# Stick-breaking attention: score matmuls two heads ahead, in pairs over four PSUM banks

## What is computed

```python
z = jnp.einsum('bhqd,bhkd->bhqk', qb, kb).astype(jnp.float32) * scale
mask = k_pos < q_pos
log_keep = jnp.where(mask, jax.nn.log_sigmoid(-z), 0.0)
after = lax.cumsum(log_keep, axis=3, reverse=True) - log_keep
w = jnp.where(mask, jnp.exp(jax.nn.log_sigmoid(z) + after), 0.0)
outs.append(jnp.einsum('bhqk,bhkd->bhqd', w.astype(vb.dtype), vb))
```

## Time and profile before

| | us |
|---|---|
| median of 3 runs | 1062.97 |
| lowest, highest | 1062.87, 1064.98 |
| span of the profiled execution | 1061.0 |
| TensorE busy | 1022.0 (96%) |
| VectorE busy | 690.2 (65%) |
| ScalarE busy | 621.5 (59%) |
| scores of the heads, first and last start | 501.1, 582.5 |

### The profile page before, as it was taken

How to read it: one execution, slowest core, us unless ns; L and a number is a source line. 1 busy time by engine, 2 the same in 40 slices (tenths; PEclk the granted TensorE clock), 3 DMA queues, 4 the chain that set the end, 5 groups by cost and what they waited for, 6 DMA issues and landing times. The chain is left out here.

```text
span 1061.0 us, 16887 instructions
## 1 busy us (share of the span) xinstructions
PE 1022.0 (96%) x6975; PEld 919.7 (87%) x6975; DVE 690.2 (65%) x981; ACT 621.5 (59%) x952; POOL 126.1 (12%) x119
## 2 busy tenths in 40 slices
PE   6999998999999999999999999999999989999997
PEld 5999897988998888789888799999889969899995
DVE  5788676867865687786566564545557886545554
ACT  6779676655664666375666654344456965443443
POOL 1010059440200122530000000000000100000000
PEclk9999999999999999899999999999999999999999
DMA  9885255433677432246332375565554355555540
GB/s 338 303 264 174 68 167 189 159 121 95 197 246 268 160 119 81 80 138 214 125 120 80 120 236 178 181 199 176 181 159 159 119 159 199 199 183 179 193 159 40
DMA packets 116476, 178.41 MB, mean 168 GB/s; under 512 B 5204, under 2 KB 74098, under 8 KB 116400
## 3 DMA queue, kind: packets, MB, share of 16 engines
q1 hardware_dynamic: 115136, 174.23, 50.1%
q0 software_dynamic: 1120, 2.97, 0.9%
q10 hardware_dynamic: 144, 0.13, 0.0%
HBM read 176.27 MB, written 1.05 MB: 167 GB/s over the span
## 5 line engine op out<-in xcount | busy, mean ns | idle before, releaser
L1484 DVE TENSOR_TENSOR sb_w_lo<-sb_raw,sb_w_hi 128x2048 fp32r<-128x2048 f32 (+1 forms) x139 | 309.4, 2227 | 194.3 <-ACT sb_w_hi L776 194.1
L776 ACT ACTIVATE sb_w_hi<-sb_raw 128x2048 fp32r<-128x2048 f32 (+1 forms) x134 | 254.2, 1900 | 135.4 <-PE G L2332 106.3
L2330 PE MATMUL X<-sb_hT_hi,sb_w_hi 128*128 128x256 f32 x784 | 222.9, 284 | 1.4 <-DVE sb_w_lo L1484 0.8
L2331 PE MATMUL X<-sb_hT_lo,sb_w_hi 128*128 128x256 f32 x784 | 221.3, 282 | 0.0
L2332 PE MATMUL X<-sb_hT_hi,sb_w_lo 128*128 128x256 f32 x784 | 221.2, 282 | 0.0
L2330 PEld LDWEIGHTS X<-sb_hT_hi,sb_w_hi 128*128 128x128 f32 x784 | 149.4, 190 | 3.3 <-issue 0.9
L2331 PEld LDWEIGHTS X<-sb_hT_lo,sb_w_hi 128*128 128x128 f32 x784 | 149.4, 191 | 0.7
L2332 PEld LDWEIGHTS X<-sb_hT_hi,sb_w_lo 128*128 128x128 f32 x784 | 149.4, 191 | 0.0
L2330 PE MATMUL G<-sb_w_hi,sb_uT_hi 128*128 128x512 f32 x304 | 121.0, 398 | 3.2 <-DVE sb_uT_lo L2265 1.6
L2332 PE MATMUL G<-sb_w_hi,sb_uT_lo 128*128 128x512 f32 x304 | 120.1, 395 | 0.0
L2331 PE MATMUL G<-sb_w_lo,sb_uT_hi 128*128 128x512 f32 x304 | 120.0, 395 | 0.0
(11 more groups left out here) (508 smaller groups left out, 1971.6 us busy)
## 6 DMA issues: line engine op xcount, KB each, us to landing
sb_raw<-in_mlp_w SPq DMA_DIRECT2D x64, 1024.0 KB, 5.2
sb_raw<-in_ada_w SPq DMA_DIRECT2D x22, 1024.0 KB, 5.4
sb_raw<-in_b_in_w SPq DMA_DIRECT2D x16, 1024.0 KB, 5.7
sb_raw<-in_a_in_w SPq DMA_DIRECT2D x14, 1024.0 KB, 6.6
sb_raw<-in_sb_w_qkv SPq DMA_DIRECT2D x12, 1024.0 KB, 5.1
sb_raw<-in_rg_w_in SPq DMA_DIRECT2D x8, 1024.0 KB, 5.3
sb_raw<-in_a_out_w SPq DMA_DIRECT2D x4, 1024.0 KB, 5.1
sb_raw<-in_b_out_w SPq DMA_DIRECT2D x4, 1024.0 KB, 5.3
```

The costliest lines, as they stand in the source:

```text
L776: nc.scalar.activation(split_tile(w_hi, m)[:, 0:nk * w], raw_of(b)[:, 0:nk * w], ACT.Copy).then_inc(S["w_hi"], 1)
L1484: ins = nc.vector.tensor_tensor(split_tile(w_lo, m)[:, at], raw_of(b)[:, at], split_tile(w_hi, m)[:, at].bitcast(F32), ALU.subtract)
L2330: dt32(out, lh, rh, start=first, stop=False, skip_group_check=shared)
L2331: dt32(out, lh, rl, start=False, stop=False, skip_group_check=shared)
```

## The change

Scores are issued two heads ahead and in pairs. `z_scores(h)` now serves heads h and h + 1: first both 256-column matmuls, then both 128-column ones, then both masks. The table `SB_AHEAD` says at the top of which iteration which pair is issued: pairs 2, 4, 6, 8, 10 at heads 0, 2, 4, 6, 8, pair 12 at head 11, pair 14 at head 12; pair 0 goes ahead of the whole V block. The banks are G0, G1, T0, T1 in turn for heads 0 to 11 and G0 to G3 for heads 12 to 15 (`z_bank`). As T0, T1, G2 and G3 are also the outputs of `sb_o`, its pieces wait for the weights of heads 10, 11, 14 and 15. The table of pieces gives the heads from 10 on fewer: one each for heads 10 to 14, pieces 28 and 29 behind the sums of head 15, and 30 and 31 behind the last product. On ScalarE the weights of head h - 1 come in iteration h, behind the high part of h and the softplus of h + 1; the two V copies of the start come behind the softplus of head 1. Splits, reads and the `o2` steps move by an iteration; the last `sb_read` stands at head 11, ahead of `z_first(12)`.

```diff
@@ -44,9 +44,11 @@
 SB_FIRST, SB_LATER = (0, 4, 1, 5), (2, 6, 3, 7)
-SB_PIECES = (3, 3, 3, 2, 2, 2, 2, 2, 2, 2, 2, 2, 2, 1, 1, 1)
-SB_SPLITS = (1, 2, 4, 6, 8, 10, 12)
-SB_READ = (2, 3, 9, 10)
+SB_PIECES = (3, 3, 3, 2, 2, 2, 2, 2, 2, 2, 1, 1, 1, 1, 1, 0)
+SB_SPLITS = (2, 3, 5, 7, 9, 11, 15)
+SB_READ = (2, 3, 9)
+SB_LAST_READ = 11
+SB_AHEAD = {0: 2, 2: 4, 4: 6, 6: 8, 8: 10, 11: 12, 12: 14}
...
@@ -492,6 +494,9 @@
...
             return (qS if n < 4 else kS)[:, 2 * (n % 4):2 * (n % 4) + 2, :], HD ** -0.5 if n < 4 else 1.0
+
+        def z_bank(h):
+            return (G[0:2] + TB)[h % 4] if h < 12 else G[h - 12]
...
@@ -1289,7 +1294,7 @@
...
                     act.wait_ge(S["sb_pv"], h - 1)
-                nc.scalar.activation(ws[h % 2][:, :, :], G[h % 2][:, 0:384].rearrange("p (c n) -> p c n", c=3),
+                nc.scalar.activation(ws[h % 2][:, :, :], z_bank(h)[:, 0:384].rearrange("p (c n) -> p c n", c=3),
...
@@ -1305,21 +1310,24 @@
...
             ch.link(nc.scalar.activation(neg_r[:, :], const("neg_ones"), ACT.Copy))
-            sb_values(0, 0)
             z_softplus(0)
-            sb_values(0, 1)
-            split_for(first_mm["sb_v"] + 1)
...
                     z_softplus(h + 1)
-                sb_weights(h)
-                if h in (5, 7):
-                    sb_values(1, (h - 5) // 2)
+                if h == 0:
+                    sb_values(0, 0)
+                    sb_values(0, 1)
+                    split_for(first_mm["sb_v"] + 1)
+                else:
+                    sb_weights(h - 1)
+                if h in (6, 7):
+                    sb_values(1, h - 6)
...
                     split_for(first_mm["sb_qk2"] + SB_SPLITS.index(h))
-                if h >= 2 and h % 2 == 0:
-                    o2_hi(h // 2 - 1)
+                if h >= 3 and h % 2 == 1:
+                    o2_hi((h - 3) // 2)
+            sb_weights(BH - 1)
...
@@ -2125,13 +2133,13 @@
...
                     dve.wait_ge(S["z_lo"], h - 1)
-                nc.vector.tensor_scalar(es[h % 2][:, :, :], G[h % 2][:, 0:384].rearrange("p (c n) -> p c n", c=3), 30.0,
+                nc.vector.tensor_scalar(es[h % 2][:, :, :], z_bank(h)[:, 0:384].rearrange("p (c n) -> p c n", c=3), 30.0,
...
                 dve.wait_ge(S["z_ln"], h + 1)
-                nc.vector.tensor_tensor(es[h % 2][:, :, :], G[h % 2][:, 0:384].rearrange("p (c n) -> p c n", c=3),
+                nc.vector.tensor_tensor(es[h % 2][:, :, :], z_bank(h)[:, 0:384].rearrange("p (c n) -> p c n", c=3),
...
@@ -2155,6 +2163,8 @@
...
                 z_second(h)
+                if h == SB_LAST_READ:
+                    sb_read(7)
...
@@ -2164,8 +2174,10 @@
...
                     split_for(first_mm["sb_qk2"] + SB_SPLITS.index(h - 1))
-                if h >= 3 and h % 2 == 1:
-                    o2_low((h - 3) // 2)
+                if h >= 4 and h % 2 == 0:
+                    o2_low((h - 4) // 2)
+            split_for(first_mm["sb_qk2"] + SB_SPLITS.index(BH - 1))
+            o2_low(KC - 2)
...
@@ -3094,23 +3106,27 @@
...
-                if h >= 2:
-                    pe.wait_ge(S["w_exp"], h - 1)
+                if h >= 4:
+                    pe.wait_ge(S["w_exp"], h - 2)
...
                     pe.wait_ge(S["fm_out"], 19 + h // 2 + 2)
-                r = half_rows(h)
-                bank = G[h % 2]
-                dt32(bank[:, 0:T], kS[r, h // 2, 0:P], qS[r, h // 2, :], start=True, stop=True, skip_group_check=True)
-                dt32(bank[:, T:3 * P], kS[r, h // 2, P:T], qS[r, h // 2, P:T], start=False, stop=True,
-                     skip_group_check=True)
-                diagonal = bank[:, 0:3 * P].rearrange("p (c n) -> p c n", c=3)[:, 0:3:2, :]
-                dt32(diagonal, sb_mask[:, 0:P], sb_mask[:, P:3 * P].rearrange("p (c n) -> p c n", c=2), start=False, stop=True,
-                     skip_group_check=True).then_inc(S["z_head"], 1)
+                pair = (h, h + 1)
+                for g in pair:
+                    r = half_rows(g)
+                    dt32(z_bank(g)[:, 0:T], kS[r, g // 2, 0:P], qS[r, g // 2, :], start=True, stop=True, skip_group_check=True)
+                for g in pair:
+                    r = half_rows(g)
+                    dt32(z_bank(g)[:, T:3 * P], kS[r, g // 2, P:T], qS[r, g // 2, P:T], start=False, stop=True,
+                         skip_group_check=True)
+                for g in pair:
+                    diagonal = z_bank(g)[:, 0:3 * P].rearrange("p (c n) -> p c n", c=3)[:, 0:3:2, :]
+                    dt32(diagonal, sb_mask[:, 0:P], sb_mask[:, P:3 * P].rearrange("p (c n) -> p c n", c=2), start=False,
+                         stop=True, skip_group_check=True).then_inc(S["z_head"], 1)
...
                 pe.wait_ge(S["z_lo"], h + 1)
-                bank = G[h % 2]
+                bank = z_bank(h)
...
@@ -3132,16 +3148,12 @@
...
-            def first_head():
-
-                pe.wait_ge(S["rows_in"], 80)
-                z_scores(0)
-
-            _, hi, lo = take()
+
+            pe.wait_ge(S["rows_in"], 80)
             for half in range(2):
-                if half == 1:
-                    first_head()
-                    _, hi, lo = take()
+                if half == 0:
+                    z_scores(0)
+                _, hi, lo = take()
...
@@ -3179,6 +3191,8 @@
...
                     n, m, pair = b - 6, p // 2, p % 2
+                    if pair == 0:
+                        pe.wait_ge(S["w_exp"], 11 + 4 * n + m)
...
@@ -3192,8 +3206,8 @@
...
             for h in range(BH):
-                if h + 1 < BH:
-                    z_scores(h + 1)
+                if h in SB_AHEAD:
+                    z_scores(SB_AHEAD[h])
...
@@ -3201,9 +3215,14 @@
...
                     piece += 1
+                if h == BH - 1:
+                    sb_piece(28)
+                    sb_piece(29)
...
             sb_pv(BH - 1)
+            sb_piece(30)
+            sb_piece(31)
...
```

## The result

| | before | after |
|---|---|---|
| median of 5 runs, us | 1063.20 | 1057.55 |
| lowest, highest | 1062.87, 1064.98 | 1057.01, 1059.11 |
| span of the profiled execution | 1061.0 | 1055.8 |
| scores 0 or V block to second half of `sb_o` | 495.44 to 590.53 | 495.85 to 586.35 |

The ratio after to before is 0.9948, with a 95% interval of 0.9937 to 0.9959: 5.5 us faster, where 2.65 were forecast and 1058.8 was the low end of the range. The forecast leaned towards a gain too small to measure; the gain is twice as large. The last row is the stretch in which the heads run, 95.1 us before and 90.5 after.

What follows compares the result with a forecast made beforehand. What TensorE issues was taken to bound the stage, except at its end. Scores -6.0, old stalls -2.2, new waits +2.55, +2.2 and +0.5, restarts +0.3 gave -2.65 us, so 1060.3 us; range 1058.8 to 1065.8.

Steps and rivals of the forecast that it cites:

- What a score pair costs: Scores on TensorE: eight pairs at 1.38 us replace 17.0 us of single heads, saving 6.0 us.
- the walk through the queue: Inside a pair: in-order issue lets halves overlap only partly, 0.85 us in place of 1.28.
- The bound of 1.16: A score pair's time if the two row halves overlapped fully: 1.16 us.
- No overlap: Rival at the score pairs: halves never run side by side, pairs cost 1.81 us, total 1063.4 us; chance 0.24.
- drains: Rival inside score pairs: each change of half empties the array, 0.20 us each, total 1068.0 us; chance 0.08.
- Old stalls: At the last heads: two sums' waits, with restarts and some tenths elsewhere, all go, saving about 2.2 us.
- Piece 24: At head 11: TensorE newly waits for the weights of head 10, idling 2.55 us.
- Scores 14: At head 12: TensorE newly waits for the weights of head 11, idling 2.2 us.
- rival 1: Clock falls in a new stall at heads 11 or 12: +1.25 us (first) or +3.45 (second); chance 0.20 with overlap.
- sb_read(7): The last read, moved to head 11, ends 0.2 to 0.3 us before scores 12 want it, so no wait.
- V copy: At the start: piece 0 waits for ScalarE to copy V out of G2, TensorE idling 0.5 us.
- What follows is TensorE-bound and shifts along.: Behind the heads: later work just moves earlier with the saving, no further gain or loss counted.

Runs made afterwards that it cites:

- e2: The changed kernel with both heads of each pair read from rows 0 to 63, order, shapes, banks and waits unchanged; median 1061.33 us.
- e10: e9 with the first V copy ahead of the softplus of head 1 on ScalarE; median 1052.60 us.
- e4: The changed kernel with pieces 30 and 31 ahead of the product of head 15, not behind it; median 1058.15 us.
- e5: The changed kernel with weights of head 10 ahead of head 12's softplus on ScalarE, and scores 14 not waiting for weights of head 11; median 1057.46 us.
- e9: e5 with the two last weight splits run after head 15's sums, not at heads 11 and 15; median 1052.54 us.
- e1: The changed kernel with each pair's scores issued one head after the other, not in turn; median 1063.56 us.
- e8: The changed kernel with only the wait of scores 14 for the weights of head 11 removed; median 1057.20 us.
- e11: The changed kernel with only the two last weight splits moved behind head 15's sums; median 1056.74 us.
- e6: e5 with the weight split of head 11 run at head 13; median 1058.58 us.
- e7: e6 with the first V copy ahead of the softplus of head 1 on ScalarE; median 1058.41 us.
- e3: The changed kernel with the weights of head 10 ahead of the softplus of head 12 on ScalarE; median 1058.29 us.

## Why the prediction was wrong, step by step

- **What a score pair costs.** This term of the sum was mis-sized: 1.38 us forecast, 1.18 measured, 1.6 us over eight pairs. The step that failed is the walk through the queue, "the other half can start only beside the second of them". The starts come two by two, at 520.44 and 520.76 us. What else a pair holds was right: 0.31 us for the ways in and out (e2: 1.83 with eight instructions in a row, 1.80 summed), 0.21 for the masks. The bound of 1.16 was in the text, and I chose against it without a row. Of the Trainium skill, TensorE: Matmul & The Clock Gate, Part 3, I used only that matmuls start and end in program order. The same part draws matmuls on different rows starting about 4 ns apart, and the starts two by two in the trace agree with that picture: both of the first two have started by 520.46 us.
- **No overlap, and drains.** Both rivals are out: e2 gives 1.83 without overlap against 1.18, and a pair with changes of half costs less than one with none. The Trainium skill says in TensorEngine Tiling (Array Packing), Key Properties, that a change of tiling mode, not just of tile, drains the engine; the trace agrees, with 0.54 us for the four.
- **Old stalls.** Right: both waits on `es_lo` are gone. From start to start they were 1.7 us of the 2.2. e10, with one short wait left, bears out the rest: its heads less that wait (0.3 us), plus 7.6 us for scores one by one, are 92.7 us, 2.4 below the 95.1 of the kernel before.
- **Piece 24.** Right in place and cause, 2.17 idle for 2.55. The prediction took the distance from log to weights from the earlier trace rows, 0.76 us; here it is 0.52 us.
- **Scores 14.** Forecast 2.2, measured 0.32 plus 1.35 of slow work. With the clock up, in e2, the wait was 1.68. As rival 1 said, a fall in the first stall fills the second. Rival 1 was given a chance of 0.20 and a cost of 1.25 us; its total was off by the other terms.
- **sb_read(7).** The prediction gave it 0.2 to 0.3 us to spare; scores 12 waited 0.28 us for it. It starts behind `z_second(11)`, which waits for a split and two o2 parts.
- **V copy.** Right, 0.55 us for 0.5.
- **"What follows is TensorE-bound and shifts along."** Wrong by 1.1 us. The prediction had listed pieces 28 to 31 as moved and then counted them at nothing. Moving two of them behind the last product lets the residual's chain run ahead, and a stall of the next stage goes (e4).

From the forecast of -2.65: -1.6 (pairs), -0.4 (piece 24), -1.9 (scores 14), +1.35 (clock), +0.4 (`sb_read(7)`), -1.1 (behind the heads) is -5.9. The traces show -5.7 from the last matmul ahead of the heads to the one behind those transposes, and 0.3 us came back ahead of the heads. The 0.2 us between are not placed.

There is a deeper fault. The sum took the two new waits as separate costs of TensorE. From scores 12 on they are one quantity, the length of the chain over the other two engines less TensorE's own work: e5 removed both and gained nothing, since a third wait and the slow clock behind it took their place. The split was the rest of it: with both edits and the split out of the chain, the way from scores 12 to sums 15 fell from 16.95 to 12.7 us (e9). Had the prediction followed `es_lo` through heads 12 to 15 with the split in it, it would have had one number for both, and the split as the thing to move. It did walk "the same chain to weights 15" and found 0.2 us to spare at sums 15, and it is there that the chain and TensorE meet.

## What to carry to other kernels

Here two fp32 products with 64 rows each, on different halves and into different banks, cost as much as one when they were issued in turn: look for such neighbours, and bring them together even at the price of one more bank each. When two waits lie near each other behind the same chain, price the chain to its last link, not the waits; and before moving an order of instructions around, ask which work in the chain is not part of it, here a weight split that was done at 571.0 us and first used at 586.35. Work moved behind an engine's last handover is not neutral: look at the first wait of the next stage.

## What the runs showed of the hardware that I had not expected

- Four fp32 instructions of 256 columns on alternating halves take 0.54 us to the next shape, on one half 0.97. The four of 128 columns behind them take 0.32 us against 0.54.
- The length of the idle alone does not decide whether the clock falls. It fell behind idles of 1.21 us (e1, ending at 441.8), 1.41 (e5), 1.68 (e2, second stall), 2.17 (after, e4, e8, e11), 2.81 (e6, e7) and 3.71 (e3), but not behind 2.16 (e2, first stall), 1.69 and another 1.21 (e1, at the heads) and 1.63. It fell inside the idle in some traces (after, e7) and up to 1.9 us behind its end in others (e1, e5). How long it stayed low differs too: 3.4 us in most, 6.8 us in e2 and e7, as in the earlier trace rows. Windows of e2 in its first idle (568.9 to 571.1 us), behind it, and in and behind its second, of 1.68 us (length, TensorE busy, granted clock, DMA share, GB/s):

```profile
570.00:571.00 1.00, 0.00 (x0) 1.00 0.00 0
...
572.00:573.00 1.00, 1.00 (x7) 1.00 0.02 8
575.00:576.00 1.00, 0.34 (x2) 1.00 0.00 0
576.00:577.00 1.00, 1.00 (x4) 0.58 0.06 16
...
582.00:583.00 1.00, 1.00 (x5) 0.50 0.00 0
583.00:584.00 1.00, 1.00 (x7) 1.00 0.00 0
```

- A fall of the clock need not cost anything. In the changed kernel the stalls at heads 11 and 12 and the slow work are 2.17 + 0.32 + 1.35 = 3.84 us; in e2, where the clock stayed up between them, the two stalls are 2.16 + 1.68 = 3.84 us. TensorE lost the same, standing or slow, as the other engines set when it could go on. Where nothing later holds TensorE, a fall costs in full: from sums 15 to the second half of `sb_o` it is 7.6 us in the changed kernel and in e9, 9.1 in e6 and 9.95 in e7, whose clock was low there for 3.4 and 5.2 us of work.

Left open: whether the overlap needs separate banks, as both heads in one bank was not tried; which of e5's two edits e9 needs beside the late splits; and what decides whether the clock falls behind an idle.
